# Retention's norm moved token-major with transposes back, rotary halves exchanged a load or two sooner, the wide convolution's taps dealt out one by one

## What is computed

```python
# layers 0 and 1, per head of 128 value columns, 4 heads
scores = einsum('bhncd,bhnmd->bhncm', qc, kc) * decay      # q, k after rotary
o = scores @ v                                             # (B,S,H,dv)
def head_groupnorm(o):
    mu = jnp.mean(o, axis=-1, keepdims=True)
    oc = o - mu
    return oc * lax.rsqrt(jnp.mean(oc * oc, axis=-1, keepdims=True) + EPS)
y_ret = (jax.nn.silu(g_ret) * o.reshape(B, S, 512)) @ w_ret_out
glu = cf_a * jax.nn.sigmoid(cf_b)
c = causal_dwconv(glu, cf_conv_w, cf_conv_b)               # K = 31, depthwise
# rotary, all layers
concatenate([x1 * cos - x2 * sin, x2 * cos + x1 * sin])
```

## Time and profile before

| what | value |
|---|---|
| median of 3 runs | 3251.43 us (3251.33 to 3252.12) |
| the profiled execution | 3251.79 us; its span 3250.4 us |
| TensorE matmul busy | 3211.3 us, 99% of the span |
| VectorE | 1830.5 us, 56% |
| ScalarE | 1234.6 us, 38% |
| GpSimd | 373.3 us, 11% |
| mean granted TensorE clock | 0.996 of full speed |

### The profile page before, as it was taken

One profiled execution on the slowest core, in us unless ns is written; L12 is line 12 of the kernel. 1 busy time (PEld: TensorE's weight loads), 2 busy tenths in 40 slices (PEclk: granted clock), 3 DMA queues, 4 the chain that ended last, 5 costly groups with the idle time before them and its releaser, 6 DMA issues.

```text
span 3250.4 us, 36847 instructions
## 1 busy us (share of the span) xinstructions
PE 3211.3 (99%) x14980; PEld 2670.7 (82%) x14980; DVE 1830.5 (56%) x2387; ACT 1234.6 (38%) x1838; POOL 373.3 (11%) x288
## 2 busy tenths in 40 slices
PE   8999999999999999999999999999999999999999
PEld 7788888888878888888887888888888788888887
DVE  3785456565477645666556643447545654345754
ACT  3232343344322333333444432226634442224642
POOL 0111111110011121111012000110012100011001
PEclk9999999999999999999999999999999999999999
DMA  4223332236422323222642222222342222222222
GB/s 159 80 78 104 98 110 85 97 105 209 148 91 72 104 95 106 87 95 98 211 137 79 80 97 94 94 85 93 101 135 75 70 95 92 93 99 91 91 94 99
DMA packets 97094, 335.49 MB, mean 103 GB/s; under 512 B 11712, under 2 KB 11968, under 8 KB 96160
## 3 DMA queue, kind: packets, MB, share of 16 engines
q1 hardware_dynamic: 93600, 318.56, 29.4%
q0 software_dynamic: 3328, 14.59, 1.3%
HBM read 326.29 MB, written 2.10 MB: 101 GB/s over the span
## 4 chain that ended last, share of the span: by engine, by line
PE 95%; DVE 3%; issue 1%; DMA 1%; SPq 0%; ACT 0%; POOL 0%; DVEq 0%; POOLq 0%
PE ps L466 94%; DVE f L1382 1%; DVE wl L1358 1%; PE ps L801 1%; PE ps L572 1%; SPq L2087 0%; DVE r L1368 0%; DMA raw<-wst 0%; DVE f L1583 0%; DMA f<-f 0%; ACT wh L914 0%; DVE f L1477 0%; POOL sm L1925 0%; ACT f L995 0%; DVE r L1740 0%
## 5 line engine op out<-in xcount | busy, mean ns | idle before, releaser
L466 PE MATMUL ps<-h,wh 128*128 128x512 f32 (+1 forms) x5824 | 1706.4, 377 | 3.2 <-DVE wl L1358 1.1
L466 PEld LDWEIGHTS ps<-h,wh 128*128 128x128 f32 x5824 | 1067.6, 189 | 203.0 <-issue 8.7
L466 PE MATMUL ps<-h,wl 128*128 128x512 f32 (+1 forms) x2912 | 1094.2, 376 | 0.0
L1358 DVE TENSOR_TENSOR wl<-raw,wh 128x1024 fp32r<-128x1024 f32 (+3 forms) x596 | 753.6, 1276 | 359.3 <-ACT wh L914 358.4
L914 ACT CAST wh<-raw 128x1024 fp32r<-128x1024 f32 (+3 forms) x596 | 594.8, 1008 | 713.9 <-PE ps L466 702.4
L466 PEld LDWEIGHTS ps<-h,wl 128*128 128x128 f32 x2912 | 549.3, 189 | 99.4
L466 PE MATMUL ps<-r,wh 128*128 128x512 f32 x1632 | 504.1, 390 | 0.0
L466 PEld LDWEIGHTS ps<-r,wh 128*128 128x128 f32 x1632 | 305.7, 188 | 62.9
L466 PE MATMUL ps<-r,wl 128*128 128x512 f32 x816 | 317.5, 389 | 0.0
L988 ACT CAST r<-f 128x512 fp32r<-128x512 f32 x182 | 112.1, 620 | 508.6 <-DVE f L1661 148.8
L466 PE MATMUL ps<-wh,r 128*128 128x512 f32 x960 | 302.6, 390 | 0.3
(11 more groups left out here) (147 smaller groups left out, 2083.9 us busy)
## 6 DMA issues: line engine op xcount, KB each, us to landing
raw<-wst SPq DMA_DIRECT2D x544, 512.0 KB, 3.3
raw<-wst SPq DMA_DIRECT2D x48, 320.0 KB, 2.9
f<-gains POOLq DMA_DIRECT2D x6, 1024.0 KB, 5.2
raw<-wst SPq DMA_DIRECT2D x16, 384.0 KB, 3.1
f<-f SPq DMA_DIRECT2D x72, 64.0 KB, 2.0
f<-tab POOLq DMA_DIRECT2D x16, 256.0 KB, 4.2
X<-x_in SPq DMA_DIRECT2D x4, 512.0 KB, 7.5
f<-gmb POOLq DMA_DIRECT2D x4, 512.0 KB, 4.5
```

Source lines behind the costliest of these rows:

```text
L466: return e.matmul(o, a, b, start=start, stop=stop, skip_group_check=True)
L1358: e.tensor_tensor(l[:, 0:WIDTH[c]], raw[:, c % NRAW, 0:WIDTH[c]], h[:, 0:WIDTH[c]].bitcast(F32), ALU.subtract).then_inc(*lo_cut.up(("lo", c)))
```

## The change

**Norm.** TensorE now multiplies scores by `v` with the score block as the stationary operand, so `o` comes out with positions on the partitions and a head's 128 values along the row. A step `ret_norm` for each head: VectorE takes four `bn_stats` of 128x128 from PSUM, four `bn_aggr` and two 128x4 operations; GpSimd the power -0.5 of 128x4 and a product of 128x4; ScalarE four `Identity` activations of 128x128 with scale and bias from PSUM to SBUF. A step `ret_turn`: TensorE transposes the four blocks back. `ret_out` then multiplies by the gate from the transposes' PSUM bank and splits. The steps `centre`, `ret_squares` and `ret_root`, and GpSimd's product in `ret_out`, are gone.

**Taps.** `tap_plan` gives every chunk from `ca2` on a number of single taps (one channel tile, one instruction): 5 for each of the four chunks `ca2` to `cb3`, 4 from `q0` to `v3`, 1 for each `g`, 2 for each `sc, sx, sb`, then 4, until all 120 are done at the 38th chunk.

**Rotary.** In layers 0 and 1 VectorE's sine product stands ahead of the `v` slot instead of behind it, and heads 0 and 1 wait for `roped` 1 only. In layers 2 and 3 the exchanges of tiles 1, 2 and 3 are issued one chunk's load sooner. (The list that the loop reads: the n-th number is the load ahead of which tile n is exchanged.)

```diff
+def tap_plan(L):
+
+    t, left = {}, {}
+
+    def some(chunk, n):
+        for _ in range(n):
+            j = max(left, key=lambda j: (left[j], -j))
+            left[j] -= 1
+            t.setdefault(chunk, []).append((left[j], j))
+
+    def first(chunk, *tiles):
+        for j in tiles:
+            t.setdefault(chunk, []).append((30, j))
+            left[j] = 30
+
+    for c in range(34):
+        chunk = NAME[f"{L}/ca2"] + c
+        if c in (0, 2, 4):
+            first(chunk, *((0, 1), (2,), (3,))[c // 2])
+        some(chunk, 5 if c < 4 else 4 if c < 12 else 1 if c < 16 else 2 if c < 28 else 4 if c < 32 else 0)
+    c = 32
+    while any(left.values()):
+        some(NAME[f"{L}/ca2"] + c, min(4, sum(left.values())))
+        c += 1
+    return t
...
-        put(t, f"{L}/sc0", [[], [("centre", L, 3)], [("ret_squares", L)], [("ret_root", L)]]
-            + [[("ret_out", L, h)] for h in range(4)])
-        put(t, f"{L}/q0", [[("tap", L, k)] for k in range(30, -1, -1)])
+        for chunk, taps in tap_plan(L).items():
+            t.setdefault(chunk, []).extend(("tap", L, i, j) for i, j in taps)
+        put(t, f"{L}/sc0", [[("ret_norm", L, 3), ("ret_out", L, 2)], [], [("ret_turn", L, 3)], [("ret_out", L, 3)]])
...
-    for _r, _n in enumerate((7, 8, 9, 10) if _L < 2 else (10, 11, 12, 12, 7)):
+    for _r, _n in enumerate((7, 8, 9, 10) if _L < 2 else (10, 10, 11, 11, 7)):
...
-                if what == "centre":
-                    o = take(("cm", L, i))
-                    w.wait_ge(*at("o", L, i))
-                    mm(o, ones, F(40 + i), True, True).then_inc(*group_done.up(("done", ("cm", L, i))))
-                elif what == "ret_root":
-                    columns(("rcol", L), [F(62 + h) for h in range(4)], at("r_square", L, 3))
-                elif what == "ret_out":
-                    rows(("rrow", L, i), small(1), 4 * i, NT, 0, at("root", "ret", L))
+                if what == "ret_turn":
+                    o = take(("rt", L, i))
+                    w.wait_ge(*at("landed", "cst"))
+                    for n in range(NT):
+                        w.wait_ge(*at("r_norm", L, i, n))
+                        last = e.transpose(o[:, n * P:(n + 1) * P], F(40 + i)[:, n * P:(n + 1) * P], ident)
+                    last.then_inc(*group_done.up(("done", ("rt", L, i))))
...
-                    if h:
-                        small_step("centre", L, h - 1)
                     pr = slice(64 * (h % 2), 64 * (h % 2) + 64)
-                    w.wait_ge(*at("roped", L, 3))
+                    w.wait_ge(*at("roped", L, 1 if h < 2 else 3))
                     for i in range(NT):
                         o = take(("qk", L, h, i))
                         mm(o[:, 0:S - P * i], F(50 + h // 2)[pr, i * P:(i + 1) * P], F(48 + h // 2)[pr, i * P:S], True,
                            True).then_inc(*group_done.up(("done", ("qk", L, h, i))))
                     o = take(("o", L, h))
-                    for i in range(NT):
-                        w.wait_ge(*at("v", L, i))
-                        w.wait_ge(*at("decayed", L, h, i))
-                        last = mm(o[:, i * P:S], F(58 + i)[:, h * P:(h + 1) * P],
-                                  scored(h % 2)[:, TRI[i]:TRI[i] + S - P * i], i == 0, i == NT - 1)
+                    for t in range(NT):
+                        w.wait_ge(*at("v", L, t))
+                        w.wait_ge(*at("decayed", L, h, t))
+                        for i in range(t + 1):
+                            c = TRI[i] + (t - i) * P
+                            last = mm(o[:, t * P:(t + 1) * P], scored(h % 2)[:, c:c + P], F(58 + i)[:, h * P:(h + 1) * P],
+                                      i == 0, i == t)
                     last.then_inc(*group_done.up(("done", ("o", L, h))))
+                    if h:
+                        small_step("ret_turn", L, h - 1)
...
+                elif what == "ret_norm":
+                    rs = small(2 + i % 2)
+                    w.wait_ge(*at("r_shift", L, i))
+                    for n in range(NT):
+                        ts = slice(n * P, (n + 1) * P)
+                        e.activation(F(40 + i)[:, ts], bank(("o", L, i))[:, ts], ACT.Identity, bias=rs[:, 4 + n:5 + n],
+                                     scale=rs[:, n:n + 1]).then_inc(*act_tile.up(("r_norm", L, i, n), ("free", ("o", L, i))))
                 elif what == "ret_out":
-                    hi_part(F(62 + i), R(40 + i), at("r_out", L, i), ("ret_hi", L, i))
+                    hi_part(F(64 + i % 2), R(40 + i), at("r_out", L, i), ("ret_hi", L, i))
...
-                    copied(("o", L, h), F(40 + h), ("o", L, h))
+                    if h:
+                        small_step("ret_norm", L, h - 1)
+                    if h > 1:
+                        small_step("ret_out", L, h - 2)
...
+                    s = 30 - i
+                    w.wait_ge(*at("tap", L, i + 1, j))
+                    C = F(20 + j)[:, s:S]
+                    e.scalar_tensor_tensor(out=C, in0=F(16 + j)[:, 0:S - s], scalar=vec1(L, "cfw", 31 * j + i)[:, 0:1],
+                                           in1=C, op0=ALU.mult, op1=ALU.add).then_inc(*dve_tap.up(("tap", L, i, j)))
+                elif what == "ret_norm":
+                    st, mv = sm2[:, i % 2, 0:24], sm2[:, i % 2, 24:40]
+                    w.wait_ge(*at("done", ("o", L, i)))
+                    for n in range(NT):
+                        e.bn_stats(st[:, 6 * n:6 * n + 6], bank(("o", L, i))[:, n * P:(n + 1) * P]).then_inc(
+                            *dve_col.up(("r_stats", L, i, n)))
+                    for n in range(NT):
+                        w.wait_ge(*at("r_stats", L, i, n))
+                        e.bn_aggr(mv[:, 2 * n:2 * n + 2], st[:, 6 * n:6 * n + 6]).then_inc(
+                            *dve_col.up(("r_moments", L, i, n)))
+                    w.wait_ge(*at("r_moments", L, i, 3))
+                    both = mv[:, 0:8].rearrange("p (n k) -> p k n", k=2)
+                    e.tensor_scalar(mv[:, 8:12], both[:, 1, :], EPS, None, ALU.add).then_inc(
+                        *dve_col.up(("col", "ret", L, i)))
+                    e.tensor_scalar(mv[:, 12:16], both[:, 0, :], -1.0, None, ALU.mult).then_inc(
+                        *dve_col.up(("r_mean", L, i)))
+                elif what == "ret_out":
+                    key, q = ("rt", L, i), F(64 + i % 2)
...
+                    swapped(L, c, 53)
                     slot(f"{L}/v{c}")
-                    swapped(L, c, 53)
...
+                    if h > 1:
+                        small_step("ret_out", L, h - 2)
...
+                if what == "ret_norm":
+                    mv, rs = sm2[:, i % 2, 24:40], small(2 + i % 2)
+                    if i > 1:
+                        w.wait_ge(*at("r_norm", L, i - 2, 3))
+                    root(mv[:, 8:12], rs, NT, at("col", "ret", L, i), ("root", "ret", L, i))
+                    w.wait_ge(*at("root", "ret", L, i))
+                    w.wait_ge(*at("r_mean", L, i))
+                    e.tensor_tensor(rs[:, 4:8], mv[:, 12:16], rs[:, 0:4], ALU.mult).then_inc(
+                        *pool_col.up(("r_shift", L, i)))
```

More of the change, by code:

```diff
@@ L1377, in small_step @@
                 if what == "tap" and i < 30:
-                    for j in range(4):
-                        s = 30 - i
-                        w.wait_ge(*at("tap", L, i + 1, j))
-                        C = F(20 + j)[:, s:S]
-                        e.scalar_tensor_tensor(out=C, in0=F(16 + j)[:, 0:S - s],
-                                               scalar=vec1(L, "cfw", 31 * j + i)[:, 0:1], in1=C, op0=ALU.mult,
-                                               op1=ALU.add).then_inc(*dve_tap.up(("tap", L, i, j)))
-                elif what == "centre":
-                    key = ("cm", L, i)
-                    w.wait_ge(*at("done", key))
-                    e.scalar_tensor_tensor(out=F(40 + i), in0=bank(key), scalar=-1.0 / P, in1=F(40 + i), op0=ALU.mult,
-                                           op1=ALU.add).then_inc(*dve_tile.up(("centred", L, i), ("free", key)))
-                elif what == "ret_root":
-                    col(("rcol", L), 16, P, small(0), ("col", "ret", L))
-                elif what == "ret_out":
-                    key = ("rrow", L, i)
-                    w.wait_ge(*at("r_prod", L, i))
-                    w.wait_ge(*at("done", key))
-                    e.tensor_tensor(F(62 + i), F(62 + i), bank(key), ALU.mult).then_inc(
@@ new lines, in small_step @@
+                    s = 30 - i
[21 more added lines that the diff above has]
+                    key, q = ("rt", L, i), F(64 + i % 2)
+                    w.wait_ge(*at("done", key))
+                    e.tensor_tensor(q, F(44 + i), bank(key), ALU.mult).then_inc(
@@ L1927, in small_step @@
             def small_step(what, L=None, i=None, j=None):
-                if what == "ret_root":
-                    root(small(0), small(1), 16, at("col", "ret", L), ("root", "ret", L))
```

(12 more changed lines are left out.)

16 lines of the change are left out of this document (5 added, 11 removed).

## The result

The changed kernel takes 3212.12 us (median of 4 runs, 3211.81 to 3212.74). The kernel before took 3251.77 us beside it (4 runs, 3251.33 to 3252.97). The ratio is 0.988, with a 95% interval of 0.986 to 0.990. So the change takes off 39.7 us; the span of the profiled execution fell from 3250.4 to 3210.5 us, by 39.9.

A forecast was written before the change was run, and what follows sets the result against it. TensorE bounds the kernel, with matmuls covering 3211.3 of 3250.4 us. The terms 21.5 - 6.1 + 3.8 + 8.2 + 10.4 = 37.8 us gave 3214 us; forecast's own range 3209 to 3220, overall 3208 to 3229.

The forecast's parts named there:

- `centre`, `columns`, `rows` off TensorE: Retention norm's matmuls in layers 0 and 1 go: 0.87 us eight times, 3.63 twice, 0.90 eight times; 21.5 us.
- transposes: Four added on TensorE for each retention head, 0.44 us a head, 3.5 us in all.
- ten pieces, new small wait: Retention's products with `v`: shorter pieces add 1.4 us, waiting for VectorE's decays 0.15 us a head, 1.2 us.
- waits at head 0: TensorE's 0.5 us for the rotary and 1.4 us for the decay both go; 3.8 us over two layers.
- waits at the scores: Two waits of 4.1 us for low parts in layers 2 and 3 go through earlier exchanges; 8.2 us.
- clock: Four half-clock stretches, one in each of layers 0 to 3, go; 10.4 us, with 0 as other bound.
- the additions: Extra TensorE time from transposes, shorter product pieces and a new small wait at retention's heads; 6.1 us together.
- the scores still wait: Rival, layers 2 and 3: VectorE and GpSimd side by side shrink the chain too little; 3228 or 3224 us; chance 0.12.
- The norm: Helper engines' chain for head h-1, some 6 us in a row, stays hidden: 8 against nearly 10 us.

The follow-up runs named there:

- turn_twice: The changed kernel with the four transposes of each head issued twice into the same bank; 3215.75 us.
- by_scores: The changed kernel with the ten products of a head run through by score block instead of by position, read for time alone; 3212.20 us.
- taps_only: The kernel before with the new tap plan, sine product ahead of the v slots in layers 0 and 1, and new `roped` wait; 3244.87 us.
- norm_only: The changed kernel with the old taps (four at each chunk from q0), sine products, `roped` wait and exchange order; 3233.97 us.
- swap_only: The kernel before with only the exchanges of layers 2 and 3 issued sooner; 3241.97 us.
- norm_late: The changed kernel with VectorE's norm of head h-1 moved behind the decays of head h (heads 1 to 3); 3232.10 us.
- columns_back: The changed kernel with 16 one-column matmuls put back ahead of the last head's transposes in layers 0 and 1; 3221.37 us.

## Why the prediction was right, and where it was off

It said 3214 us, and 3212.1 was measured: 37.8 us of gain against 39.7. Term by term:

| term | predicted | measured |
|---|---|---|
| `centre`, `columns`, `rows` off TensorE | 21.5 | 21.6: 0.86, 3.63 and 0.93 each |
| transposes | -3.5 | -3.5: 0.43 a group in a head, 0.45 the last; 0.46 in turn_twice |
| ten pieces, new small wait | -2.6 | -0.6: 0.08 a head (4.61 - 4.53 at head 0; by_scores: no wait in it) |
| waits at head 0 | 3.8 | 3.8 |
| waits at the scores | 8.2 | 8.2, less 0.4 of new wait |
| clock | 10.4 | 10.4: 3.0, 1.6, 3.1 and 2.7 |
| in no term | | 0.7 of stalls gone, 0.5 lost at the start |

With the last row this is 39.7 of the 39.9 us between the two spans.

**The term that was mis-sized** is the additions, 6.1 where 4.1 was measured. The prediction took for the ten products the pace of `rows`, which have float32 pieces of 128x128 between other work, and added 0.15 us for a wait. A head shows neither. The lower bounds given there, nothing for both, were nearly the truth. The row was the wrong kind: ten pieces in a row with the columns of four cost little more than the columns do.

**`columns` at 3.63** is the length of a record, which is not how TensorE's pace was to be read, and it came out all the same. The next matmul starts 3.49 us on (177.46 to 180.95), but those behind it come late too. From the sums to `rows` it is 9.07 us, and the chunk between them is 5.44 by the prediction's pace: 3.63 for the sums. Read in this way `rows` is 0.93 (186.53 to 192.90, less a chunk), 0.03 more than between two `wl` starts.

**The range** had a gap in its working: the lower bounds that it names, no small wait and no cost of the pieces, take 2.6 us off 3214.0 and give 3211.4, not 3209. The 3212.1 lies just inside what its own terms can give.

**The clock** is the term with the thinnest ground: the prediction took half of each stretch at half clock as lost. It can be read by itself, since each stretch with a fall has one without a fall that does the same work. Head 0 before, in layer 0 (with a fall) and in layer 1 (without), from the scores to `centre`:

```profile
118.01 2.42 PE L466 MATMUL ps<-f,f 64*128 64x512 f32 x8 [0.51 <-POOL f L1981]
...
132.52 1.02 PE L466 MATMUL ps<-f,ct 128*128 128x512 f32 x2
...
941.24 2.42 PE L466 MATMUL ps<-f,f 64*128 64x512 f32 x8 [0.52 <-POOL f L1981]
...
952.74 1.02 PE L466 MATMUL ps<-f,ct 128*128 128x512 f32 x2
```

This is 14.51 us against 11.50: 3.0 us. The first scores of layer 2 before, and the transposes behind two chunks:

```profile
1749.53 6.21 PE L466 MATMUL ps<-r,r 128*128 128x128 f32 x20 [4.09 <-DVE r L1740]
...
1764.69 1.25 PE L801 MATMUL ps<-ct,f 128*128 128x128 f32 x10
```

It is 15.16 us, and 12.04 in after (1718.92 to 1730.96): 3.1 us. In layer 3 it is 14.73 (2538.90 to 2553.63) against 12.04 (2501.28 to 2513.32): 2.7 us. Behind the sums of layer 1 it is 10.66 (997.68 to 1008.34) against the 9.07 of layer 0: 1.6 us. So the sizes were right. Whether a fall comes is another matter. The profiled executions of all nine kernels give:

| what TensorE did before | cases | followed by a fall |
|---|---|---|
| waited 4 us or more at the scores (before, taps_only, norm_only) | 6 | 6 |
| waited 0.5 and 1.4 us at head 0 (before, swap_only, norm_only) | 6 | 5 |
| waited 1.4 to 2.5 us at a head (norm_late) | 6 | 3 |
| 16 one-column sums (before, swap_only, taps_only, columns_back) | 8 | 6 |
| a head without a wait (after, by_scores, turn_twice) | 24 | 0 |
| waited 0.5 and 0.6 us at a layer boundary (all nine) | 18 | 0 |

The kernel before leaves six places of the first, second and fourth kind in an execution and fell at four in its trace. The changed kernel leaves none, and its time also varies less: the kernel before had medians of 3251.8, 3253.7 and 3253.8 us in three sets of runs, the changed one 3212.1 and by_scores, its twin in time, 3212.2. So how near 37.8 came to the measured gain is in part luck: against the other two medians the gain is some 41.6 us. What decides between fall and no fall at one place wasn't found. One of the four runs of the changed kernel (3212.74) had a mean granted clock of 0.999 where the others have 1.000, so a fall somewhere in it isn't ruled out.

The granted clock is 1.00 with four and with eight transposes in a row. The Trainium skill ("TensorE: Matmul & The Clock Gate", Part 4: PE-mode transpose) says that transposes don't count as busy for the clock in the way that matmuls do. By that rule they could have brought falls; behind transposes that TensorE hadn't waited for there was none in the traces of after, by_scores and turn_twice.

Four `bn_stats` of 128 elements took 0.89 us. The Trainium skill ("VectorE: DVE Perf Modes", the TRN2 errata) says that small tiles pay a fixed cost each. The trace agrees as far as it goes: 0.22 us for 128 elements is more than a quarter of the 0.64 us that another operation takes for 512, and TensorE never waited for it.

**The waits at the scores went, but with less to spare.** The prediction left 1.6 us. Timelines after, layer 2: SyncE (the exchanges of tiles 2 and 3), VectorE (two sine products, the splits, the low parts for the scores), TensorE (the first scores):

```profile
1703.81 4.95 SPq L2130 DMA_DIRECT2D f<-f  x8
```

```profile
1709.64 2.38 DVE L1621 TENSOR_TENSOR f<-f,f 128x512 f32<-128x512 f32 x2
1712.05 3.38 DVE L1400 TENSOR_TENSOR r<-f,r 64x512 fp32r<-64x512 f32 x2
1715.46 1.81 DVE L1390 TENSOR_TENSOR wl<-raw,wh 128x640 fp32r<-128x640 f32 x1
1717.18 1.28 DVE L1780 TENSOR_TENSOR r<-ps,r 128x512 fp32r<-128x512 f32 x2
```

```profile
1718.92 2.41 PE L493 MATMUL ps<-r,r 128*128 128x128 f32 x16
```

The low parts end at 1718.46, 0.46 us ahead of TensorE; in layer 3 it is 0.51 us (2500.77 and 2501.28). Of the slack 0.5 us went since the two sine products take 1.2 us each, where the prediction had 0.7 for the first. And 1.0 us went where the prediction had reserved it, beside GpSimd: the split of 128x640 took 1.81 us where it had been 0.83 us (at 1747.40 before). It began at 1715.46, when GpSimd's last sum (L2025, 1714.96 to 1716.58) was already running; before, that sum had ended first. The rival "the scores still wait" had its mechanism right and missed by half a microsecond.

**The norm** was early, as said: no wait at any of the eight groups, even behind four taps (norm_only). Its chain on VectorE and GpSimd took 2.8 us where the prediction counted about 4.5 (the nearest row, 0.29 us for a reduction, was too dear for `bn_stats`, and GpSimd's second operation takes 0.20 us and not 1). What it then waits for is the sigmoid ahead of it on ScalarE. The prediction named this order and put no time on it; it is 3.2 us, and still ends in time.

**What was in no term.** In the kernel before TensorE also starts a chunk late once in each of layers 0 and 1, by 0.4 us at 247.66 and 0.3 at 1069: in layer 0 VectorE's split of that chunk, behind four taps, ends at 247.56. Both stalls are gone in after. Against that TensorE's first matmuls lost 0.5 us more (see below). And the wait for the low parts in layer 2 of norm_only is 5.1 us instead of 4.1, as SyncE's eight issues took 5.92 us there (from 1718.19) instead of 4.94; why they did stays open.

## What to carry to other kernels

Where one engine is busy for 99% of the span, count what a change puts on and takes off it, from start to start of two rows and not from a record's length, with the second row a chunk further on where the matmuls behind come late too, and check the helpers' chain only against the moment at which that engine asks. Means over features that TensorE makes by matmuls with ones can go to VectorE in the other layout: here the transposes back and the shorter products cost 4.1 us for 21.6 taken off. A wait on TensorE may cost twice, since the clock may fall behind it: removing a wait of 1.4 us brought 3.0 us more in layer 0 and nothing more in layer 1, and the time also varied less from run to run.

## What was not expected of the hardware

- The clock's falls are not tied to the instructions alone. Behind the same 16 one-column sums it fell in 6 of 8 cases, with everything ahead of them in layer 0 unchanged between before (none) and swap_only (0.66).
- A fall can start inside the light work. In taps_only the one-column sums of layer 0 took 4.03 us instead of 3.63, and the window 175 to 180 us was granted 0.51.
- The windows don't show the slow start. In after, three matmuls of 256 columns take 0.64 us up to 23.16 us from the span's start and 0.36 from there on, and the granted clock stands at 1.00 in both stretches. The change of pace comes at 21.5 to 24.7 us in the nine traces (22.3 before, 23.2 after), which is where the 0.5 us above went, and it differs between executions of the same first instructions.
- Ten plain float32 products of 128 columns cost 0.08 us more than four with the same columns in all.
- What a split costs beside GpSimd depends on which began first. The traces of before and after have 82 splits of 128x640 or 128x1024 beside an operation of GpSimd on 128x512, where both stand in rows of their own. The 44 that began ahead of it took about their usual 0.83 or 1.22 us. The 38 that began while it ran all took longer, up to 1.81 us (128x640) and 2.32 us (128x1024).
